# Gate units of a two-block transformer kernel computed in pairs by seven quarter products

## The chip, the cores and the metric

The kernel runs on one core of one Trainium2 chip. The metric is device time in microseconds, the median of several executions. The core's engines run side by side, each with its own queue of instructions, and wait for each other on semaphores: TensorE (PE in the profile; its weight loads are PEld), VectorE (DVE), ScalarE (ACT), GpSimd (POOL) and SyncE (SP), which issues the transfers of the weights.

## The reference, cut to what matters

Two transformer blocks run one after the other on 512 tokens of width 1024: a first block (stick-breaking attention, cross-attention, convolutional feed-forward) and a second with three branches (an RWKV-7 recurrence, a short convolution, a pooling). Only the end of the second block is touched. There `p_gate` holds 3 x 1024 columns of `h @ w_in`:

```python
y_a, v_layer = rwkv7_branch(...)
y_b = short_conv_branch(p_conv, conv_w[l])
y_c = pool_branch(p_pool, pool_w[l], pool_scale[l])
ys = jnp.stack([y_a, y_b, y_c], axis=0)
proj = jnp.einsum('nbsc,ncd->nbsd', ys, w_branch[l])
gates = jax.nn.sigmoid(p_gate.reshape(bsz, slen, N_BRANCH, D_MODEL))
merged = jnp.einsum('bsnd,nbsd->bsd', gates, proj)
out = merged @ w_out[l]
x = x + rms_norm(out, post_norm_w[l])
```

## The kernel before

**Tiles and units.** Activations lie transposed, features on the 128 partitions and the 512 tokens along the free dimension: `x_hi` and `x_lo` are eight such blocks. A *unit* is the weights of 128 output features, 1024 input rows deep, as a tile of 128x1024 (512 KB). 217 units are read in the order of their use, unit `u` into place `u % 4` of `stage`. SyncE issues the transfer of unit `u` when TensorE has finished unit `u - 4` (line 516).

**Three products for one.** Everything is split in two fp32r parts to keep fp32 accuracy. ScalarE rounds half a unit (128x512) from `stage` to `w_hi` (`split_hi`, line 1448). GpSimd subtracts (`split_lo`, line 2075) and writes `w_lo`, which lies at the same address as `stage`: the remainder replaces the weights. `product` (lines 562 to 564) then issues for each of a unit's eight blocks `w_lo` with `x_hi`, `w_hi` with `x_lo`, `w_hi` with `x_hi`, 24 matmuls of 512 columns into one bank of PSUM.

**The end of the second block.** After the recurrence come sixteen units "conv" (lines 1340 to 1342), eight units "pool", thirty-six units "branch" and eight units "out". VectorE makes the convolution's result (`conv_out`, lines 2825 to 2833), and for "pool" a windowed sum by doublings (lines 2877 to 2881); TensorE multiplies that with a small matrix (`mix`, line 1386, an fp32 product that the trace shows as x2), VectorE scales it (`pool_out`, line 2865), ScalarE rounds it (`pool_hi`, line 1993) and GpSimd makes the remainder (`pool_lo`, line 2240).

The branch stage has twelve steps, three branches by four pairs of output tiles. A step has three units: two gate units (output features `2m` and `2m + 1`), whose results ScalarE turns into `gates` by a sigmoid (line 2015), and one unit that holds both tiles' branch weights (24 matmuls, lines 1417 to 1419). VectorE multiplies gate and projection (line 2896) and adds to `Y` (line 2899). In the last four steps ScalarE rounds finished tiles of `Y` (`merged_hi`, line 2027) and GpSimd makes their remainders (`merged_lo`, line 2257) for "out". The first two units of "out" are computed interleaved, block by block (`two_products`, lines 579 to 592), so both must be ready when "out" begins.

Each engine's order is its program, written by hand as below. ScalarE splits unit `b + d + 2` ahead of the sigmoid of unit `b + d`; GpSimd goes through the units in order, three ahead.

## Time and profile before

| | |
|---|---|
| three runs | 1420.45, 1421.04, 1421.90 us; median 1421.04 us |
| span of the profiled execution | 1418.9 us, first to last instruction |
| TensorE busy | 1399.4 us, 99% |
| GpSimd, VectorE, ScalarE busy | 757.9, 666.8, 657.0 us |
| branch stage | about 1166 to 1363 us |

The profiled execution's own device time isn't listed. Its span is 2.1 us under the median of the runs, which is what lies around the span. Percentages of busy time are means over stages that differ much: TensorE is busy throughout, while the others wait for it for long in the branch stage.

### The profile page before, as it was taken

How to read it: one execution, taken by the hardware profiler on the slowest of the kernel's cores; microseconds unless marked ns; L12 is line 12 of the kernel's file. 1: busy time of each engine (PE TensorE's matmuls, PEld its weight loads, DVE VectorE, ACT ScalarE, POOL GpSimd, SP SyncE). 2: the span in 40 equal slices, each digit the busy share in tenths (PEclk: the TensorE clock that was granted, in tenths of full speed). 3: DMA queues.
4: the chain of work that ended last, by engine and by line, in shares of the span. 5: the costliest groups of instructions: out<-in, count | busy, mean ns of one | idle time of the engine just before them, and what ended most of it. 6: DMA issues, size and time to landing. Idle time of an engine off the chain costs nothing.

```text
span 1418.9 us, 23591 instructions
## 1 busy us (share of the span) xinstructions
PE 1399.4 (99%) x9244; PEld 1158.8 (82%) x9244; DVE 666.8 (47%) x857; ACT 657.0 (46%) x1138; POOL 757.9 (53%) x601
## 2 busy tenths in 40 slices
PE   8999999999999999999999999999999999999998
PEld 6888888787889888888888887788878878888887
DVE  5566655547646433333454875544355352111222
ACT  6555555535446544443332467456553333222343
POOL 4444433356346665656666545954337645445562
PEclk9999999999999999999999999999999999999999
DMA  5222222132131222232333312200023322323232
GB/s 211 90 88 77 87 75 84 65 104 75 60 134 45 80 99 98 95 99 94 105 104 104 119 45 89 75 19 3 3 74 120 103 89 89 105 89 104 89 103 75
DMA packets 34218, 122.99 MB, mean 87 GB/s; under 512 B 3792, under 2 KB 4304, under 8 KB 34000
## 3 DMA queue, kind: packets, MB, share of 16 engines
q1 hardware_dynamic: 33408, 119.51, 25.0%
q10 hardware_dynamic: 720, 2.20, 0.4%
q8 instruction: 67, 1.10, 0.3%
q14 instruction: 23, 0.19, 0.0%
HBM read 119.59 MB, written 2.10 MB: 86 GB/s over the span
## 4 chain that ended last, share of the span: by engine, by line
PE 87%; DVE 5%; issue 3%; ACT 3%; POOL 1%; DMA 0%; SPq 0%; POOLq 0%; ACTq 0%; DVEq 0%
PE ps L562 18%; PE ps L563 18%; PE ps L564 18%; PE ps L1340 2%; PE ps L1341 2%; PE ps L1342 2%; PE ps L1419 2%; PE ps L1418 2%; PE ps L1417 2%; PE ps L684 1%; PE ps L669 1%; POOL w_lo L2075 1%; PE ps L697 1%; PE ps L1106 1%; PE ps L849 1%
## 5 line engine op out<-in xcount | busy, mean ns | idle before, releaser
L2075 POOL TENSOR_TENSOR w_lo<-stage,w_hi 128x512 fp32r<-128x512 f32 x422 | 592.3, 1427 | 495.2 <-ACT w_hi L1448 495.1
L562 PE MATMUL ps<-x_hi,w_lo 128*128 128x512 f32 x888 | 349.6, 394 | 0.0
L564 PE MATMUL ps<-x_hi,w_hi 128*128 128x512 f32 x888 | 346.0, 390 | 0.0
L563 PE MATMUL ps<-x_lo,w_hi 128*128 128x512 f32 x888 | 345.8, 389 | 0.0
L1448 ACT ACTIVATE w_hi<-stage 128x512 fp32r<-128x512 f32 x422 | 241.6, 622 | 61.5 <-DMA stage<-w 53.8
L562 PEld LDWEIGHTS ps<-x_hi,w_lo 128*128 128x128 f32 x888 | 166.7, 188 | 36.6 <-issue 1.2
L564 PEld LDWEIGHTS ps<-x_hi,w_hi 128*128 128x128 f32 x888 | 166.7, 188 | 34.9
L563 PEld LDWEIGHTS ps<-x_lo,w_hi 128*128 128x128 f32 x888 | 166.8, 188 | 34.7 <-issue 1.2
L2567 DVE SCALAR_TENSOR_TENSOR conv<-ps,vcol,conv 128x511 f32<-128x511 f32 x44 | 33.0, 749 | 132.8 <-ACT conv L1668 132.8
L1668 ACT ACTIVATE conv<-ps,vcol 128x512 f32<-128x512 f32 x44 | 34.2, 778 | 121.4 <-PE ps L564 120.4
L2896 DVE TENSOR_TENSOR bt<-gates,ps 128x512 f32<-128x512 f32 x24 | 16.3, 679 | 141.5 <-PE ps L1419 141.5
L2015 ACT ACTIVATE gates<-ps 128x512 f32<-128x512 f32 x24 | 14.3, 597 | 114.2 <-PE ps L564 114.2
L562 PE MATMUL ps<-f_hi,w_lo 128*128 128x512 f32 x154 | 59.9, 389 | 0.0
L563 PE MATMUL ps<-f_lo,w_hi 128*128 128x512 f32 x154 | 59.9, 389 | 0.0
L564 PE MATMUL ps<-f_hi,w_hi 128*128 128x512 f32 x154 | 59.9, 389 | 0.0
L2115 POOL TENSOR_TENSOR f_lo<-conv,f_hi 128x512 f32 (+1 forms) x22 | 28.5, 1296 | 43.9 <-ACT f_hi L1680 43.9
L1340 PE MATMUL ps<-x_hi,w_lo 128*128 128x512 f32 x128 | 51.1, 400 | 0.1
L1341 PE MATMUL ps<-x_lo,w_hi 128*128 128x512 f32 x128 | 49.8, 389 | 0.0
L1342 PE MATMUL ps<-x_hi,w_hi 128*128 128x512 f32 x128 | 49.8, 389 | 0.0
L2187 POOL TENSOR_TENSOR Mk<-blk,levels 128x256 f32<-128x256 f32 x40 | 28.5, 728 | 38.1 <-PE ps L1276 17.4
L2319 DVE SCALAR_TENSOR_TENSOR keep<-ps,soft 128x1280 f32<-128x1280 f32 x16 | 23.8, 1490 | 42.5 <-ACT soft L1494 42.2
L1417 PE MATMUL ps<-ys_hi,w_lo 128*128 (+1 forms) x96 | 37.8, 393 | 0.0
(476 smaller groups left out, 2862.3 us busy)
## 6 DMA issues: line engine op xcount, KB each, us to landing
stage<-w SPq DMA_DIRECT2D x211, 512.0 KB, 3.3
extra_stage<-w SPq DMA_DIRECT2D x6, 512.0 KB, 5.1
H<-xT SPq DMA_DIRECT2D x4, 512.0 KB, 7.3
mem<-memT SPq DMA_DIRECT2D x2, 512.0 KB, 10.8
pool_n<-pool_count ACTq DMA_DIRECT2D x1, 1024.0 KB, 5.5
outT<-outs SPq DMA_DIRECT2D x4, 256.0 KB, 2.4
outT<-outs SPq DMA_DIRECT2D x2, 384.0 KB, 3.0
w_small<-small ACTq DMA_DIRECT2D x1, 512.0 KB, 5.8
```

Of the source, the lines that this page charges most:

```text
L562: pe.matmul(out, wl, hi(k), start=first, stop=False)
L563: pe.matmul(out, wh, lo(k), start=False, stop=False)
L564: mm = pe.matmul(out, wh, hi(k), start=False, stop=end)
L1340: pe.matmul(o, wl, x_hi[:, k, :], start=(k == 0), stop=False)
L1341: pe.matmul(o, wh, x_lo[:, k, :], start=False, stop=False)
L1342: mm = pe.matmul(o, wh, x_hi[:, k, :], start=False, stop=(k == KB - 1))
L1417: pe.matmul(o, wl, hi, start=(k == 0), stop=False)
L1448: act.activation(unit_hi(b)[:, cols], unit_stage(b)[:, cols], ACT.Copy).then_inc(whi_made, 1)
L1668: act.activation(conv[:, t % UP_BANKS, :], ps[:, t % UP_BANKS, :], ACT.Identity, scale=V("ffn_conv", (4 + t % 2) * FFB + p), bias=V("ffn_c ...
L2075: pool.tensor_tensor(unit_lo(b)[:, cols], unit_stage(b)[:, cols], unit_hi(b)[:, cols].bitcast(F32), ALU.subtract).then_inc(wlo_made, 1)
L2115: pool.tensor_tensor(f_lo[:, p, :], conv[:, slot, :], f_hi[:, p, :].bitcast(F32), ALU.subtract).then_inc(ff_made, 1)
L2567: dve.scalar_tensor_tensor(out=conv[:, j, 1:SEQ], in0=ps[:, j, 0:SEQ - 1], scalar=tap(1), in1=conv[:, j, 1:SEQ], op0=ALU.mult, op1=ALU.add ...
```

## The change

The two gate units of a step are one product of 256 output features, 1024 inputs and 512 tokens. The change cuts it in quarters: the weights by output tile and by half of the inputs (A11 and A12 are the halves of the first unit, A21 and A22 of the second), `x` by half of the inputs and half of the tokens. Eight quarter products are replaced by seven (the form of Strassen's scheme with fifteen sums), each four blocks deep and 256 columns wide.

- Four sums of `x` (`t_val`, `t_hi`, `t_lo`, 128x1024 each) are made once, in the conv stage: eight operations and four remainders on VectorE, four roundings on ScalarE.
- For each pair VectorE makes four 128x512 sums of weights (`pair_sums`), one of them in place in `stage`. ScalarE rounds three of them and GpSimd makes their remainders (`sum_hi`, `sum_lo`). The half A11, whose remainder overwrites `stage`, waits for the third sum.
- Three intermediate results are copied from PSUM to `gates` by ScalarE between the quarter products. VectorE adds the last parts (`gate_out`, `gate_out2`), and the sigmoid then works in place.
- The sequence of splits follows the pairs: the gate units of a pair are split only when their sums are made, one pair ahead, and the first pair after the pool stage. Other units are split as before.
- Some buffers move (`pool_n`, `sg`, `mg_hi`, `mg_lo`; `pt` and `pld` go into `cb`), and semaphores of the first stages are merged to free some; these wait for the same events as before.

```diff
+            def gate_pair(p, b, i=0, first=False):
...
+                if first:
+                    pe.wait_ge(pl_out_s, CA - 1)
+                pe.wait_ge(st_out_s, 8 * i + (2 * p + 2))
+                pe.wait_ge(wlo_made, 24 * i + (2 * b + 1))
+                seventh(B, hi0[:, left], lo0[:, left], *x_quarter(0, 0), start=True).then_inc(st_done_s, 1)
+                pe.wait_ge(wlo_made, 24 * i + (2 * b + 2))
...
+                seventh(Dq, hi1[:, right], lo1[:, right], *t_quarter(3), start=True)
                 if first:
                     mix(CA - 1)
+                pe.wait_ge(st_lo_s, 12 * i + (3 * p + 1))
+                n = s_place(0, p)
+                seventh(Cq, s_hi[n], s_lo[n], *t_quarter(0)).then_inc(st_done_s, 1)
+                pe.wait_ge(wlo_made, 24 * i + (2 * b + 3))
+                seventh(A, hi0[:, right], lo0[:, right], *x_quarter(1, 0), start=True).then_inc(unit_done, 1)
...
+                seventh(B, s_hi[n], s_lo[n], *t_quarter(1)).then_inc(st_done_s, 1)
...
+                seventh(Cq, s_hi[n], s_lo[n], *x_quarter(1, 1)).then_inc(st_done_s, 1)
+                pe.wait_ge(wlo_made, 24 * i + (2 * b + 4))
+                pe.wait_ge(st_copy_s, 12 * i + (3 * p + 3))
+                seventh(B, hi1[:, left], lo1[:, left], *t_quarter(2)).then_inc(unit_done, 1)
...
-                    split_hi(b + 2)
+                    if j < CA - 1:
+                        split_hi(b + 2)
...
+                if j == 13:
+                    for n in range(4):
+                        act.wait_ge(t_made_s, n + 1)
+                        act.activation(t_hi[n][:], t_val[n][:], ACT.Copy).then_inc(t_hi_s, 1)
...
+            def step(m, p, first=False):
...
+                act.activation(gates[:, g, 0:HS], quarter[:, 4, :], ACT.Copy).then_inc(st_copy_s, 1)
+                split_hi(b + 2)
...
+                act.activation(gates[:, g + 1, :], ps[:, 1, :], ACT.Copy).then_inc(st_copy_s, 1)
                 if first:
                     pool_hi(CA - 1)
...
+                act.activation(gates[:, g, HS:SEQ], quarter[:, 4, :], ACT.Copy).then_inc(st_copy_s, 1)
...
+                pair_hi(b + 3, 0)
+                pair_hi(b + 4, 1)
+                gate(m, p, 0)
+                sum_hi(0, p + 1)
+                sum_hi(1, p + 1)
+                pair_hi(b + 3, 1)
+                gate(m, p, 1)
+                sum_hi(2, p + 1)
+                third_hi(b + 4, p + 1)
...
+            def pair_los(p):
+                pair_lo(p, 0)
+                pair_lo(p, 1)
+                sum_lo(0, p)
+                pair_lo(p, 2)
+                sum_lo(1, p)
+                sum_lo(2, p)
+                pair_lo(p, 3)
...
             for m in range(4):
...
+                split_lo(U0["branch"] + 24 + 3 * m + 2)
+                if m < 3:
+                    pair_los(2 * QB + m + 1)
+                else:
+                    split_lo(U0["out"])
+                for k in range(2 * m - 2, 2 * m):
+                    if k >= 0:
+                        merged_lo(k)
+            split_lo(U0["out"] + 1)
             for k in range(KB - 2, KB):
                 merged_lo(k)
...
+            conv_out(1)
+            t_sums()
+            conv_out(2)
+            t_lows()
+            conv_out(3)
...
+            def pair_sums(p):
...
+                dve.wait_ge(whi_made, 2 * u + 2)
+                if p:
+                    dve.wait_ge(st_done_s, 4 * (p - 1) + 4)
+                dve.tensor_tensor(S1, A21, A22, ALU.add).then_inc(st_sum_s, 1)
+                dve.wait_ge(st_sum_s, 4 * p + 1)
+                dve.tensor_tensor(A21, A11, A21, ALU.subtract).then_inc(st_sum_s, 1)
+                dve.tensor_tensor(S2, S1, A11, ALU.subtract).then_inc(st_sum_s, 1)
+                dve.wait_ge(st_sum_s, 4 * p + 3)
+                dve.tensor_tensor(S4, A12, S2, ALU.subtract).then_inc(st_sum_s, 1)
...
+            for p in range(3 * QB):
+                gate_out(p)
+                if p < 3 * QB - 1:
+                    pair_sums(p + 1)
+                gate_out2(p)
+                taken(p)
```

**ScalarE at the end of the pool stage.** `sg<-ps` is the result of the last pool unit, `ys_hi<-cb` the rounding of the third pooled block (`pool_hi(2)`), which waits for VectorE's `pool_out` (`pl_out`). Before:

```order
L1448 ACTIVATE w_hi_51<-stage_50 128x512
L1453 ACTIVATE cb_178<-ps 128x512 [waits unit_done]
L1448 ACTIVATE w_hi_51<-stage_50 128x512 [waits landed2]
L1448 ACTIVATE w_hi_51<-stage_50 128x512
L2005 ACTIVATE sg_179<-ps 128x512 [waits unit_done]
L1993 ACTIVATE ys_hi_176<-cb_178 128x512 [waits gn_lo,pl_out]
L1448 ACTIVATE w_hi_51<-stage_50 128x512 [waits landed3]
```

After:

```order
L1514 ACTIVATE cb_178<-ps 128x512 [waits unit_done,pl_lo]
L2071 ACTIVATE sg_179<-ps 128x512 [waits unit_done]
L2058 ACTIVATE ys_hi_176<-cb_178 128x512 [waits gn_lo,pl_out]
L2079 ACTIVATE w_hi_51<-stage_50 128x512 [waits landed1]
L2079 ACTIVATE w_hi_51<-stage_50 128x512 [waits landed2]
L2085 ACTIVATE s_hi0_195<-s_val0_203 128x512 [waits st_sum]
L2085 ACTIVATE s_hi1_196<-s_val1_204 128x512 [waits st_sum]
L2079 ACTIVATE w_hi_51<-stage_50 128x512 [waits landed1]
```

The splits of the first two gate units stood ahead of `sg`; they now stand behind `ys_hi`, in four pieces with the sums' roundings between them.

**GpSimd in the last steps and ahead of "out".** `mg_lo` is the remainder of two tiles of `Y`, `w_lo` that of weights (two rows make a unit). Before, from the first `mg_lo` to the end:

```order
L2257 TENSOR_TENSOR mg_lo_184<-Y_55,mg_hi_183 128x512 [waits mg_hi_made] x2
L2075 TENSOR_TENSOR w_lo_49<-stage_50,w_hi_51 128x512 [waits whi_made] x6
L2257 TENSOR_TENSOR mg_lo_184<-Y_55,mg_hi_183 128x512 [waits mg_hi_made] x2
L2075 TENSOR_TENSOR w_lo_49<-stage_50,w_hi_51 128x512 [waits whi_made] x6
L2257 TENSOR_TENSOR mg_lo_184<-Y_55,mg_hi_183 128x512 [waits mg_hi_made] x4
L2075 TENSOR_TENSOR w_lo_49<-stage_50,w_hi_51 128x512 [waits whi_made] x12
```

After, from the last of the remainders of pair 10 on (two rows of L2190 are a whole unit; L2372 and L2380 are the seven pieces of pair 11):

```order
L2399 TENSOR_TENSOR mg_lo_182<-Y_55,mg_hi_181 128x512 [waits mg_hi_made] x2
L2190 TENSOR_TENSOR w_lo_49<-stage_50,w_hi_51 128x512 [waits whi_made] x2
L2372 TENSOR_TENSOR w_lo_49<-stage_50,w_hi_51 128x512 [waits st_sum,whi_made] x2
L2380 TENSOR_TENSOR s_lo0_199<-s_val0_203,s_hi0_195 128x512 [waits st_sum,st_hi]
L2372 TENSOR_TENSOR w_lo_49<-stage_50,w_hi_51 128x512 [waits st_sum,whi_made]
L2380 TENSOR_TENSOR s_lo2_201<-s_val2_205,s_hi2_197 128x512 [waits st_sum,st_hi]
L2380 TENSOR_TENSOR s_lo3_202<-s_val3_206,s_hi3_198 128x512 [waits st_sum,st_hi]
L2372 TENSOR_TENSOR w_lo_49<-stage_50,w_hi_51 128x512 [waits st_sum,whi_made]
L2399 TENSOR_TENSOR mg_lo_182<-Y_55,mg_hi_181 128x512 [waits mg_hi_made] x2
L2190 TENSOR_TENSOR w_lo_49<-stage_50,w_hi_51 128x512 [waits whi_made] x4
L2399 TENSOR_TENSOR mg_lo_182<-Y_55,mg_hi_181 128x512 [waits mg_hi_made] x2
L2190 TENSOR_TENSOR w_lo_49<-stage_50,w_hi_51 128x512 [waits whi_made] x2
```

Two `mg_lo` now stand ahead of the remainders of a pair's branch unit (the first and the ninth row), and the remainders of the second unit of "out" (the last row) stand behind the third pair of `mg_lo`; before they stood ahead of it.

## Rows read from the trace of the kernel before

**Rows 1.** The page: busy time of engines, and the chain that ended last.

```profile
PE 1399.4 (99%) x9244; PEld 1158.8 (82%) x9244; DVE 666.8 (47%) x857; ACT 657.0 (46%) x1138; POOL 757.9 (53%) x601
PE 87%; DVE 5%; issue 3%; ACT 3%; POOL 1%; DMA 0%; SPq 0%; POOLq 0%; ACTq 0%; DVEq 0%
```

**Rows 2.** Busy time by stretch: start:end, length, busy (instructions) of PE, PEld, DVE, ACT, POOL, granted clock.

```profile
1177.00:1363.00 186.00, 186.00 (x820) 153.68 (x820) 39.20 (x46) 54.08 (x98) 94.77 (x75) 1.00 0.29 96
1415.00:1416.00 1.00, 0.00 (x0) 0.00 (x0) 0.26 (x1) 0.38 (x1) 0.00 (x0) 1.00 0.73 279
...
1418.00:1419.00 1.00, 0.00 (x0) 0.00 (x0) 0.00 (x0) 0.00 (x0) 0.00 (x0) 0.63 0.00 1
```

**Rows 3.** Timeline of PE, 512 columns: first and last of a step's 48 gate matmuls.

```profile
1183.39 0.39 PE L562 MATMUL ps<-x_hi,w_lo 128*128 128x512 f32 x1
...
1194.05 0.39 PE L564 MATMUL ps<-x_hi,w_hi 128*128 128x512 f32 x1
```

**Rows 4.** The same, 256 columns: first and last of 36 matmuls.

```profile
785.77 0.28 PE L1035 MATMUL ps<-f_hi,w_lo 128*128 128x256 f32 x1
...
789.97 0.28 PE L1037 MATMUL ps<-f_hi,w_hi 128*128 128x256 f32 x1
```

**Rows 5.** PE, DVE, ACT and POOL where the pool stage ends.

```profile
1165.26 1.02 PE L1386 MATMUL ps<-pld,w_small 128*128 128x512 f32 x2
1165.71 0.80 PE L562 MATMUL ps<-x_hi,w_lo 128*128 128x512 f32 x1
1160.65 0.15 DVE L2877 COPY pt<-cb 128x1 f32<-128x1 f32 x1 [4.93 <-ACT cb L1453]
1167.75 0.74 DVE L2865 SCALAR_TENSOR_TENSOR cb<-ps,vcol,sg 128x512 f32<-128x512 f32 x1
1168.53 0.63 ACT L1993 ACTIVATE ys_hi<-cb 128x512 fp32r<-128x512 f32 x1 [2.47 <-DVE cb L2865]
1169.06 1.14 ACT L1448 ACTIVATE w_hi<-stage 128x512 fp32r<-128x512 f32 x2
1161.21 2.77 POOL L2075 TENSOR_TENSOR w_lo<-stage,w_hi 128x512 fp32r<-128x512 f32 x2 [0.17 <-ACT w_hi L1448]
```

**Rows 6.** SP and ACT: two gate units' transfers, from issue to the split.

```profile
1194.65 0.33 SPq L516 DMA_DIRECT2D stage<-w  x1
1197.99 1.15 ACT L1448 ACTIVATE w_hi<-stage 128x512 fp32r<-128x512 f32 x2 [1.82 <-DMA stage<-w]
...
1210.94 0.33 SPq L516 DMA_DIRECT2D stage<-w  x1
1214.67 1.15 ACT L1448 ACTIVATE w_hi<-stage 128x512 fp32r<-128x512 f32 x2 [2.18 <-DMA stage<-w]
```

**Rows 7.** POOL remainders alone and beside DVE, and DVE beside them.

```profile
1180.85 5.05 POOL L2075 TENSOR_TENSOR w_lo<-stage,w_hi 128x512 fp32r<-128x512 f32 x4
1124.65 5.94 POOL L2075 TENSOR_TENSOR w_lo<-stage,w_hi 128x512 fp32r<-128x512 f32 x4 [0.74 <-ACT w_hi L1448]
1127.78 1.66 DVE L2880 TENSOR_TENSOR pld<-pt,pool_n 128x512 f32<-128x512 f32 x1
1219.10 0.69 DVE L2899 TENSOR_TENSOR Y<-Y,bt 128x512 f32<-128x512 f32 x1
```

**Rows 8.** Groups by shape: sigmoid and 128x256 copies on ACT, 128x1024 on DVE.

```profile
L2015 ACT ACTIVATE gates<-ps 128x512 f32<-128x512 f32 x24 | 14.3, 597 | 114.2 <-PE ps L564 114.2
L1926 ACT ACTIVATE R<-ps 128x256 f32<-128x256 f32 x31 | 11.5, 385 | 13.0 <-PE ps L1276 7.1 <-PE ps L1295 4.8
L2427 DVE TENSOR_TENSOR prob<-prob,soft_sum 128x1024 f32<-128x1024 f32 x4 | 4.9, 1225 | 0.1
```

**Rows 9.** Conv stage: DVE's gap, POOL beside it, and PE at unit 12.

```profile
1093.56 0.72 DVE L2825 TENSOR_TENSOR cb<-cb 128x512 f32<-128x512 f32 x1 [14.54 <-ACT cb L1947]
1086.62 4.61 POOL L2234 TENSOR_TENSOR ys_lo<-g_sq,ys_hi 128x2048 fp32r<-128x2048 f32 x1
1098.16 0.39 PE L1340 MATMUL ps<-x_hi,w_lo 128*128 128x512 f32 x1
```

More of the change, by code:

```diff
@@ L369, in build_block @@
         xa_max = sem("xa_max")
-        xa_nmax = sem("xa_nmax")
         xa_exp = sem("xa_exp")
@@ L1396, in _, with seventh @@
                     mix(j - 1)
-            def step(n, m, b, i=0, first=False):
-                for d in range(2):
-                    pe.wait_ge(evac, 8 * i + (EV0["branch"] + 2 * ((b - U0["branch"]) // 3) + d + CREDIT - 1))
-                    product(ps[:, (U0["branch"] + d) % 2, :], 12 * i + (b + d), (b + d) % RING, x_rows, x_rows_lo)
+            def seventh(out, wh, wl, hi, lo, start=False):
+                for k in range(QB):
+                    cols = slice(k * P, (k + 1) * P)
+                    pe.matmul(out, wl[:, cols], hi(k), start=start and k == 0, stop=False, skip_group_check=True)
+                    pe.matmul(out, wh[:, cols], lo(k), start=False, stop=False, skip_group_check=True)
+                    mm = pe.matmul(out, wh[:, cols], hi(k), start=False, stop=(k == QB - 1), skip_group_check=True)
+                return mm
@@ new lines, in x_quarter, with t_quarter @@
+            def x_quarter(r, c):
+                return lambda k: x_hi[:, QB * r + k, HALF[c]], lambda k: x_lo[:, QB * r + k, HALF[c]]
+            def t_quarter(n):
+                return lambda k: t_hi[n][:, k, :], lambda k: t_lo[n][:, k, :]
+            def gate_pair(p, b, i=0, first=False):
+                left, right = (slice(0, UNIT // 2), slice(UNIT // 2, UNIT))
+                hi0, lo0, hi1, lo1 = (t[:, (b + d) % RING, :] for d in range(2) for t in (w_hi, w_lo))
+                A, Dq, Cq, B = (quarter[:, n, :] for n in (1, 2, 3, 4))
+                if first:
[4 more added lines that the diff above has]
+                pe.wait_ge(wlo_made, 24 * i + (2 * b + 2))
+                if first:
+                    pe.wait_ge(t_lo_s, 4)
+                    pe.wait_ge(evac, EV0["branch"] + CREDIT)
+                seventh(Dq, hi1[:, right], lo1[:, right], *t_quarter(3), start=True)
@@ L1406, in step @@
+            def step(n, m, b, i=0, first=False):
+                gate_pair(m, b, i, first)
                 st = (b - U0["branch"]) // 3
@@ L2016, in step @@
                 if first:
                     pool_hi(CA - 1)
-                split_hi(b + 4)
-            for m in range(4):
-                step(m, U0["branch"] + 3 * m, first=m == 0)
-            for m in range(4):
-                step(m, U0["branch"] + 12 + 3 * m)
+                act.wait_ge(st_done_s, 4 * p + 3)
+                act.activation(gates[:, g, HS:SEQ], quarter[:, 4, :], ACT.Copy).then_inc(st_copy_s, 1)
+                if not more:
+                    split_hi(b + 3)
+                    gate(m, p, 0)
+                    gate(m, p, 1)
+                    split_hi(b + 4)
+                    return
@@ L2025, in merged_hi @@
+            third_hi(b + 1, 0)
+            act.wait_ge(pl_pooled_s, CA)
+            for p in range(2 * QB):
+                step(p % QB, p, first=p == 0)
             def merged_hi(k):
@@ new lines, in gate_out, with gate_out2 @@
+            def gate_out(p):
+                g = 2 * (p % 2)
+                dve.wait_ge(st_done_s, 4 * p + 4)
+                dve.wait_ge(st_copy_s, 3 * p + 3)
+                g0 = gates[:, g, :].rearrange("p (h n) -> p h n", n=HS)
+                dve.tensor_tensor(g0, g0, quarter[:, 1:4:2, :], ALU.add).then_inc(st_out_s, 1)
+            def gate_out2(p):
+                g1 = gates[:, 2 * (p % 2) + 1, :].rearrange("p (h n) -> p h n", n=HS)
+                dve.wait_ge(unit_done, U0["branch"] + 3 * p + 2 + CREDIT)
+                dve.tensor_tensor(g1, g1, quarter[:, 4:5, :].to_broadcast([P, 2, HS]), ALU.add).then_inc(st_out_s, 1)
@@ L2903, in _ @@
-            with dve.Fori(1, 3) as i:
-                for m in range(4):
-                    step(m, U0["branch"] + 3 * m, i)
+            for p in range(3 * QB):
[4 more added lines that the diff above has]
+                taken(p)
             dve.memset(acc2[:], 0.0).then_inc(acc2_made, 1)
```

220 lines of the change are left out of this document (144 added, 76 removed).

## Prediction, made before the changed kernel was run

> **What bounds the kernel now.** First the page: TensorE is busy for 99% of the span and has 87% of the chain that ended last [rows 1], so a saved matmul counts fully as long as nothing comes late. Then the stretches: in the branch stage TensorE is busy without a gap, GpSimd for 95 us of 186, ScalarE and VectorE for less [rows 2]. So there is room beside TensorE, but room in a mean says nothing about lateness. For that I follow one step by the timeline. Last I look at the two ends of the stage, where the new preparation has no earlier pair to hide behind.
>
> The profiled execution has a span of 1418.9 us, 2.1 under the median. I work on the span and add the difference to the median, 1421.04.
>
> **What goes.** A step's gate units are 48 matmuls of 512 columns; from the first to the last, 47 intervals take 10.66 us, 0.2268 each, so 10.89 for the pair [rows 3]. The new pair is seven quarters of four blocks by three products, 84 matmuls of 256 columns. 36 of this kernel's present 256-column matmuls, with their weight loads, start 0.1200 apart [rows 4]: 10.08 us, 1.44 a quarter. That gains 0.81 a pair, 9.7 us for twelve. It isn't an eighth of 10.89 since a narrow matmul costs more than half of a wide one. A step shrinks from 16.33 to 15.52, the branch unit's 24 matmuls staying at 5.44.
>
> **The steady step** (time 0 is a pair's first quarter). ScalarE's roundings cost 0.57 to 0.62 each, GpSimd's remainders 1.263 (5.05 for four), VectorE's sums 0.69 and 0.04 between two [rows 5, 7].
> The next pair's second unit takes the place that the fourth quarter frees. A transfer is issued 0.60 after the start of the last matmul [rows 3, 6], 0.11 less with the shorter matmul: 6.13. It is being rounded 3.34 to 3.73 after the issue [rows 6]: 9.6, rounded at 10.2. VectorE needs the sixth quarter's result for `gate_out` by then (8.9 to 9.6), fits, and makes three sums: 12.4. Only now may GpSimd overwrite A11: it starts at 12.5 and has nine operations to the end of the next branch unit's remainders, 11.4 us: 23.9.
> VectorE's operations with two SBUF inputs and GpSimd's hinder each other: 0.69 became 1.66 beside GpSimd, and GpSimd's four took 5.94 for 5.05, 0.45 for each of the two VectorE operations within them [rows 7]. Three such (the fourth sum, two additions to `Y`) make 25.2. The branch unit begins at 15.52 + 10.08 = 25.60. The first remainder is ready at 13.8 to 14.2 for 15.52, and the later ones come every 1.26 to 1.7 for quarters of 1.44. So a steady step is hidden by 0.4 us at its tightest place. ScalarE's third copy, which the seventh quarter waits for, has one quarter, 1.44, for 0.39 [rows 8] and about 0.3 of waiting. I charge 1.0 for eleven steps, bounds 0 and 3 (a transfer at 3.73 in each and one more collision in some).
>
> **The first pair.** Before, ScalarE split both gate units ahead of the pool stage's last results. Now they stand behind `ys_hi`. Reckoned: the fp32 `mix` ends at 1166.28; `pool_out` takes 0.74 (VectorE is done with its doublings by then, since GpSimd's 2.77 us of splits beside them go: about 2.0 earlier), `ys_hi` 0.63, two half units 1.14, three sums 2.2, a remainder 1.27, with 0.05 to 0.1 for each handing over: 1172.5 to 1173.2 [rows 5, 7]. The upper end has a sum behind `ys_lo` and the remainder behind the fourth sum. TensorE had its first gate matmul behind `mix` at 1166.3. Stall: 6.2 to 6.9, I take 6.5. Nothing hides it; the quarter waits for these weights alone.
> The first branch unit's remainders stand behind the seven pieces and `pool_lo(3)`: 1172.6 + 7 x 1.27 + 1.3 + 2.5 = 1184.0 for 1183.7 (10.08 and 0.86 for `mix` on): 0.3, bounds 0 and 0.6.
>
> **The clock in that stall.** The trace has one long idleness of TensorE, the tail: no matmul runs from 1415.0 on, and the granted clock of 1418 to 1419 is 0.63 on average [rows 2], so within it the clock went from 2.4 GHz to 1.2 GHz. An idleness of 6.5 us is longer. I count on the fall. How long the low level then lasts isn't in these rows. At one end it costs nothing, at the other half of the first pair's 10.08 us runs at half rate, 5. I take 1.5, near the lower end, since the pair's pieces come only every 1.27 us and the waits 0.3 above would take up a part.
> The Trainium skill, "TensorE: Matmul & The Clock Gate", Part 1, says that idleness lowers the clock and that only sustained work releases it again. By that rule the term can't be zero; without it the sum below would be 1424.7. The rule speaks against this change, which makes the kernel's first long idleness in the middle of its work.
>
> **The last pairs.** Pairs are counted from 0 to 11. Behind the pieces of pairs 10 and 11 GpSimd makes two remainders of `Y` ahead of the branch unit's: 2.53 more, 27.7 for 25.6. The branch product of step 10 waits 2.1 (bounds 1.7 and 2.6). The one of step 11 gains from it: TensorE is 2.1 later, GpSimd's chain began before the wait, so it is late by about 0.
> Ahead of "out": the seventh quarter ends at 10.3, `gate_out2` 11.0, sigmoid 11.65, the split of the second unit of "out" 12.8, two tiles of `Y` rounded 13.4 and 14.1. GpSimd has its two `mg_lo` to 16.0 and then the second unit's halves: 18.6, and 0.45 to 0.9 more beside VectorE's last additions. "out" begins at 15.52 and asks for both halves 0.45 later. Late by 2.4 to 3.5; I take 3.0. Before, this split stood first.
>
> **The sums of x.** VectorE has a gap of 14.5 us behind `conv_out(1)` [rows 9]. Eight sums of 128x1024 at 1.23 [rows 8] are 9.8 alone and up to 19 beside GpSimd. Each holds GpSimd up by about 0.9; its unit 12, behind the 4.61 us remainder of `g_sq`, then ends near TensorE's start of that unit, 1098.16 [rows 9]. Charged 0.5, bounds 0 and 2.5. ScalarE's four roundings (about 1 us each) and the four `t_lo` delay `conv_out(3)` by a microsecond or two, which the pool stage's gaps of 4.9 us on VectorE take up [rows 5]. Semaphores merged and buffers moved: nothing, their waits are on the same events.
>
> **The sum.** -9.7 + 6.5 + 0.3 + 1.5 + 1.0 + 2.1 + 3.0 + 0.5 = +5.2: 1426.2 us. All terms at their lower ends give +0.6 (1421.6), all at their upper ends +14.4 (1435.4).
>
> **The rivals.**
> *Near break-even, 1422.* The same stalls at their lower ends, the clock returned at once: +0.6 to +2.8. For it: the tight places are tight by tenths. Against: four terms would have to be low together.
> *Faster, 1417.9.* GpSimd isn't late at the end: the place is its queue from pair 10 on, the price 2.1 + 3.0 of my sum. It decides if the nine remainders and two `mg_lo` end before 25.6, so if its chain starts 2.1 earlier than 12.5, that is if the second unit's weights are there at 8.1 instead of 10.2. Then only the join is left: -9.7 + 6.2 + 0.3 = -3.2. Against: transfers of 3.3 us or more in every step [rows 6].
> *Collisions in every step, 1433.* VectorE's four sums all collide and the branch product is late by 0.7 in each of the steps not yet counted: +7. Against: GpSimd is idle when the first three sums run.
> *The change doesn't do what it says, 1430.* If the narrow matmuls with new groups started 0.125 apart the gain would be 4.7. Against: [rows 4], whose weights change with each matmul too.
>
> **How the numbers follow.** This kernel's measurement tells about 0.2%, 2.8 us, from no change: 1418.2 to 1423.9 is "same". My forecast has 0.54, break-even 0.21, faster 0.11, collisions 0.09, the weaker gain 0.05. Slower by over 0.2%: 0.54 + 0.09 + 0.05 = 0.68, same 0.21, faster 0.11. Range 1418.5 to 1431.5: it leaves out most of the faster case and the upper part of the collisions.
>
> **What would show it.** In the trace after: quarter matmuls 0.120 apart, 1.44 a quarter; one idle stretch of TensorE of 6 to 7 us released by GpSimd's first `w_lo` of the branch stage, and a clock under 1.00 in or behind it; steps of 15.5 us; a wait of 2 us at the branch product of step 10 and one near 3 us at the second unit of "out"; next to nothing in the conv stage. It would be wrong if the gap at the join is short, if steady steps show waits of GpSimd's, or if the clock stays low for long.

## The result, and the profile after

The changed kernel takes 1427.93 us (median of 4 runs, 1427.56 to 1429.48) and the kernel before 1420.74 us (1419.9 to 1421.9). The ratio is 1.0053, with a 95% interval of 1.0038 to 1.0067: slower by about half a per cent. The medians differ by 7.2 us. The prediction said 1426.2 us, 1418.5 to 1431.5, slower with a chance of 0.68. The profiled execution spans 1425.6 us, 6.7 more than the 1418.9 of before.

First the page: busy time by engine, and under it the chain that ended last.

```profile
PE 1395.2 (98%) x9676; PEld 1175.5 (82%) x9676; DVE 749.9 (53%) x941; ACT 697.4 (49%) x1214; POOL 828.8 (58%) x637
PE 90%; DVE 4%; POOL 2%; ACT 2%; issue 1%; DMA 1%; SPq 0%; ACTq 0%; POOLq 0%; DVEq 0%
```

Against [rows 1]: TensorE is busy for only 4.2 us less, though the quarter products save over 9 (most of the rest is work at a lower clock, as shown below). VectorE is busy for 83 us more and GpSimd for 71. GpSimd's share of the chain is 2%, where it was 1%. Where GpSimd is waited for, the waits of TensorE say (engine, tile and line <- what it waited for: us in total, times, longest), from 1000 us to the end:

```profile
PE ps L1419 <- POOL w_lo L2372: 6.7, 1, 6.7
PE ps L607 <- POOL w_lo L2190: 2.6, 1, 2.6
PE ps L1478 <- POOL w_lo L2190: 2.1, 1, 2.1
```

All three are new, and each is for a remainder of GpSimd's: at the first pair (L1419), at the second unit of "out" (L607), and at the branch product of step 10 (L1478). Nothing else in the branch stage waits, in the steady steps not once. The steps, from the timeline of TensorE (start, duration, engine and line, tiles, in brackets the idleness before it), are the first quarter matmul of a pair (L1419) or the first of a branch unit (L1478), and last the one of "out" that waits (L607):

```profile
1221.52 0.28 PE L1419 MATMUL ps<-x_hi,w_lo 128*128 128x256 f32 x1
...
1231.59 0.40 PE L1478 MATMUL ps<-ys_hi,w_lo 128*128 128x512 f32 x1
...
1237.06 0.28 PE L1419 MATMUL ps<-x_hi,w_lo 128*128 128x256 f32 x1
...
1342.59 0.50 PE L1478 MATMUL ps<-ys_hi,w_lo 128*128 x1 [2.06 <-POOL w_lo L2190]
...
1349.78 0.28 PE L1419 MATMUL ps<-x_hi,w_lo 128*128 128x256 f32 x1
...
1368.54 0.79 PE L607 MATMUL ps<-mg_hi,w_lo 128*128 128x512 f32 x1 [2.60 <-POOL w_lo L2190]
```

A pair takes 1231.59 - 1221.52 = 10.07 us, the branch unit 5.47, the step 15.54 where it was 16.32. So each steady step is a gain, of 0.78 us. But the branch unit of step 10 takes 7.19 us from its first matmul to the next pair, 1.7 more than its sisters. The granted clock tells why. Windows of one microsecond with TensorE alone (start:end, length, busy share and matmuls, granted clock, DMA share, GB/s), around step 10 and around the join:

```profile
1344.00:1345.00 1.00, 1.00 (x5) 0.54 0.00 0
1345.00:1346.00 1.00, 1.00 (x4) 0.50 0.00 0
1346.00:1347.00 1.00, 1.00 (x3) 0.50 0.00 0
1347.00:1348.00 1.00, 1.00 (x5) 0.75 0.00 0
1348.00:1349.00 1.00, 1.00 (x6) 1.00 0.00 0
```

```profile
1169.00:1170.00 1.00, 0.00 (x0) 1.00 0.00 0
1170.00:1171.00 1.00, 0.00 (x0) 0.50 0.00 0
...
1175.00:1176.00 1.00, 1.00 (x7) 0.50 0.00 0
1176.00:1177.00 1.00, 1.00 (x7) 0.58 0.00 0
1177.00:1178.00 1.00, 1.00 (x5) 1.00 0.00 0
```

At the join the clock is at the lower of its two levels (0.50 is 1.2 GHz) from 1170 us, still within the wait, to 1176.9; TensorE works again from 1171.72. The pair takes 13.25 us to its branch unit, where 10.08 and 0.86 for the pool product are 10.94: 2.3 us more. At step 10 the fall comes 1.5 us behind the wait's end, when TensorE is already busy again. At "out" there is a third one: it comes at 1368.0, in the last half microsecond of the wait, and lasts to 1371.4; the stretch from the first product of "out" to the end takes 60.28 us for 55.99 before, of which 2.6 are the wait and 1.7 the clock.

The join itself, answering [rows 5], with all engines (the order is that of the chain):

```profile
1164.03 1.02 PE L1402 MATMUL ps<-cb,w_small 128*128 128x512 f32 x2
1165.09 0.75 DVE L3035 SCALAR_TENSOR_TENSOR cb<-ps,vcol,sg 128x512 f32<-128x512 f32 x1 [0.50 <-PE ps L1402]
1165.87 0.63 ACT L2058 ACTIVATE ys_hi<-cb 128x512 fp32r<-128x512 f32 x1 [1.05 <-DVE cb L3035]
1166.41 1.13 ACT L2079 ACTIVATE w_hi<-stage 128x512 fp32r<-128x512 f32 x2
1167.57 0.82 DVE L3063 TENSOR_TENSOR s_val<-stage 128x512 f32<-128x512 f32 x1 [1.73 <-ACT w_hi L2079]
1169.87 2.94 POOL L2372 TENSOR_TENSOR w_lo<-stage,w_hi 128x512 fp32r<-128x512 f32 x2 [2.02 <-DVE s_val L3066]
1171.72 0.55 PE L1419 MATMUL ps<-x_hi,w_lo 128*128 128x256 f32 x1 [6.67 <-POOL w_lo L2372]
```

Scaling, `ys_hi`, two half units, three sums, remainder: one after the other, as the prediction had it, and TensorE beside it idle.

### The profile page after: what moved, and what is told of

The parts are those of the page before. It is cut to its first block, busy times and chain, and to the rows that moved or that the text cites. A ratio compares the mean times of both kernels' runs of the same rounds, so it can differ in the third digit from the quotient of the medians.

```text
span 1425.6 us, 24785 instructions
## 1 busy us (share of the span) xinstructions
PE 1395.2 (98%) x9676; PEld 1175.5 (82%) x9676; DVE 749.9 (53%) x941; ACT 697.4 (49%) x1214; POOL 828.8 (58%) x637
## 4 chain that ended last, share of the span: by engine, by line
PE 90%; DVE 4%; POOL 2%; ACT 2%; issue 1%; DMA 1%; SPq 0%; ACTq 0%; POOLq 0%; DVEq 0%
PE ps L578 16%; PE ps L579 16%; PE ps L580 16%; PE ps L1419 3%; PE ps L1420 3%; PE ps L1421 3%; PE ps L1356 2%; PE ps L1358 2%; PE ps L1357 2%; PE ps L1478 1%; PE ps L1479 1%; PE ps L1480 1%; PE ps L685 1%; PE ps L713 1%; PE ps L700 1%; PE ps L950 1%
## 5 line engine op out<-in xcount | busy, mean ns | idle before, releaser
L2190 POOL TENSOR_TENSOR w_lo<-stage,w_hi 128x512 fp32r<-128x512 f32 x374 | 541.3, 1472 | 401.8 <-ACT w_hi L1509 401.6
L578 PE MATMUL ps<-x_hi,w_lo 128*128 128x512 f32 x696 | 274.6, 395 | 0.0
L580 PE MATMUL ps<-x_hi,w_hi 128*128 128x512 f32 x696 | 271.3, 390 | 0.0
L579 PE MATMUL ps<-x_lo,w_hi 128*128 128x512 f32 x696 | 271.1, 390 | 0.0
L1509 ACT ACTIVATE w_hi<-stage 128x512 fp32r<-128x512 f32 x374 | 214.0, 622 | 48.3 <-DMA stage<-w 38.1
L578 PEld LDWEIGHTS ps<-x_hi,w_lo 128*128 128x128 f32 x696 | 130.7, 188 | 28.9 <-issue 1.1
L580 PEld LDWEIGHTS ps<-x_hi,w_hi 128*128 128x128 f32 x696 | 130.6, 188 | 27.6
L579 PEld LDWEIGHTS ps<-x_lo,w_hi 128*128 128x128 f32 x696 | 130.7, 188 | 26.8 <-issue 1.0
L2372 POOL TENSOR_TENSOR w_lo<-stage,w_hi 128x512 fp32r<-128x512 f32 x48 | 67.9, 1426 | 31.7 <-DVE s_val L3066 31.7
L2380 POOL TENSOR_TENSOR s_lo<-s_val,s_hi 128x512 fp32r<-128x512 f32 x36 | 53.8, 1508 | 0.0
L1356 PE MATMUL ps<-x_hi,w_lo 128*128 128x512 f32 x128 | 51.2, 400 | 0.1
L1358 PE MATMUL ps<-x_hi,w_hi 128*128 128x512 f32 x128 | 49.9, 390 | 0.0
L1357 PE MATMUL ps<-x_lo,w_hi 128*128 128x512 f32 x128 | 49.8, 389 | 0.0
L2463 DVE SCALAR_TENSOR_TENSOR keep<-ps,soft 128x1280 f32<-128x1280 f32 x16 | 23.9, 1491 | 42.3 <-ACT soft L1555 42.1
L1478 PE MATMUL ps<-ys_hi,w_lo 128*128 (+1 forms) x96 | 38.3, 399 | 2.1 <-POOL w_lo L2190 2.1
```

The source lines that it names most:

```text
L578: pe.matmul(out, wl, hi(k), start=first, stop=False)
L579: pe.matmul(out, wh, lo(k), start=False, stop=False)
L580: mm = pe.matmul(out, wh, hi(k), start=False, stop=end)
L1356: pe.matmul(o, wl, x_hi[:, k, :], start=(k == 0), stop=False)
L1357: pe.matmul(o, wh, x_lo[:, k, :], start=False, stop=False)
L1358: mm = pe.matmul(o, wh, x_hi[:, k, :], start=False, stop=(k == KB - 1))
```

## The experiments

All are the changed kernel with one edit or several, timed beside the kernel before, in 4 to 11 executions each. They ran on two chips, and each ratio is to the kernel before on the same chip. The changed kernel itself stands at 1.0053 on this scale, and 0.1% are 1.4 us. **Theory:** the whole loss is three waits, at the two ends of the stage, and the clock's falls behind them; the steady step is the gain that it seems. **Rivals:** the cost is spread (operations of VectorE and GpSimd that hinder each other in every step), or the waits are there whatever the order, since GpSimd has too much to do.

| kernel | median, us | ratio to before, 95% | against the changed kernel | theory |
|---|---|---|---|---|
| e_out_first | 1423.89 | 1.0024 (1.0015 to 1.0033) | -4.1 | -4.3 |
| e_merged_gap | 1428.82 | 1.0061 (1.0048 to 1.0074) | +1.1 | -3.8 |
| e_join_early | 1428.13 | 1.0055 (1.0042 to 1.0068) | +0.3 | -7.8 |
| e_warm_join | 1424.85 | 1.0036 (1.0023 to 1.0049) | -2.4 | -2.3 |
| e_join2 | 1418.68 | 0.9985 (0.9976 to 0.9994) | -9.7 | -7.7 |
| e_tail | 1420.76 | 1.0004 (0.9995 to 1.0013) | -7.0 | -8.0 |
| e_all2 | 1413.52 | 0.9947 (0.9933 to 0.996) | -15.1 | -15.7 |
| e_pool_extra | 1430.1 | 1.0068 (1.0053 to 1.0084) | +2.1 | +5.4 |

The fourth column is the difference of the ratios, in microseconds of 1420.7. The changed kernel's own ratio is known to 0.15% either way, so such a difference is good to some 2.5 us: +0.3, +1.1, -2.4 and +2.1 aren't clear of nothing by the time alone, and what is said of these four rests on their traces.

### The second unit of "out" first (e_out_first)

```diff
                 else:
                     split_lo(U0["out"])
+                    split_lo(U0["out"] + 1)
                 for k in range(2 * m - 2, 2 * m):
                     if k >= 0:
                         merged_lo(k)
-            split_lo(U0["out"] + 1)
```

> One change to the changed kernel: GpSimd splits the second unit of "out" directly behind the first, ahead of its four merged_lo remainders of k = 4 to 7, as the kernel before did. In the changed kernel's trace TensorE waits 2.6 us for that unit's w_lo, and its granted clock is 0.50 in the three microseconds behind the wait; from the first product of "out" to the end takes 60.28 us, 4.29 more than before. Theory (the wait and the clock fall behind it are one cost of the order on GpSimd): both go, 60.3 falls to 56.0 to 56.6, the whole to 1423.3 to 1424.2 us. Rival (the remainders mg_lo become the late ones in its place): the wait moves to mg_lo, at least 2 us of the 4.3 stay, and the whole is 1426 or more.

The theory held: -4.1 us for the expected -4.3. From the first product of "out" to the end this trace takes 56.0 us, as before the change, and the granted clock is 1.00 for as long as TensorE works there. No remainder became late in the unit's place. So the wait at "out" came of the place of one line, not of GpSimd's load.

### The merged remainders into the idle stretch (e_merged_gap)

```diff
                 split_lo(U0["branch"] + 24 + 3 * m + 2)
+                for k in range(2 * m - 4, 2 * m - 2):
+                    if k >= 0:
+                        merged_lo(k)
                 if m < 3:
                     pair_los(2 * QB + m + 1)
                 else:
                     split_lo(U0["out"])
-                for k in range(2 * m - 2, 2 * m):
-                    if k >= 0:
-                        merged_lo(k)
+            for k in range(KB - 4, KB - 2):
+                merged_lo(k)
             split_lo(U0["out"] + 1)
```

> One change to the changed kernel: in the last block's third and fourth steps GpSimd computes the merged remainders that ScalarE has made ready in the step before (k = 0, 1 and 2, 3) in its own idle stretch, directly behind the branch unit's split, and no longer between the pair's remainders and the next branch unit. In the changed kernel's trace the branch product of step 10 waits 2.06 us for its w_lo, and takes 7.19 us where the others take 5.47, at a granted clock of 0.50. Theory: the wait and the slow product both go, 3.8 us, and the stretch from the end of the pool stage to "out" is 197.5 us where it was 201.29; the whole 1424 us. Rival (a wait of 2.1 us is too short to bring the clock down, and the slow product comes of something else, say the port): 2.1 us go, the product stays at 7.2, the whole 1425.9. Second rival (the two remainders don't fit into the gap, 3.0 us, and delay the next pair): nothing is gained.

Nothing was gained, but not for the reason that any of the three gives. The waits of TensorE in its trace:

```profile
PE ps L1419 <- POOL w_lo L2372: 6.7, 1, 6.7
PE ps L607 <- POOL w_lo L2190: 4.6, 1, 4.6
PE ps L1478 <- POOL w_lo L2190: 0.6, 2, 0.4
```

The wait at step 10 is gone (the 0.6 us are 0.2 at step 1 and 0.4 at step 11), so the remainders do fit into the gap. But TensorE now reaches "out" 2 us sooner, and the unit it needs there comes when it came: the 2.6 us became 4.6, with the clock down behind it for longer. GpSimd works there without a gap from 1345.55, where pair 11's pieces begin, to 1369.04, where that unit's remainders are done: work taken out of step 10 stands in the same queue ahead of "out". The two waits at the end are one debt, and to remove the earlier alone moves it.

### Both orders (e_tail)

```diff
                 split_lo(U0["branch"] + 24 + 3 * m + 2)
+                if m == 2:
+                    merged_lo(0)
+                    merged_lo(1)
                 if m < 3:
                     pair_los(2 * QB + m + 1)
                 else:
                     split_lo(U0["out"])
-                for k in range(2 * m - 2, 2 * m):
-                    if k >= 0:
-                        merged_lo(k)
             split_lo(U0["out"] + 1)
-            for k in range(KB - 2, KB):
+            for k in range(2, KB):
                 merged_lo(k)
```

> The two orders on GpSimd together, since e_merged_gap's trace shows the wait that it took from step 10 (2.06 to 0 us) come back whole at the second unit of "out" (2.6 to 4.6 us): both are one chain on GpSimd. Here the remainders of k = 0, 1 go into the idle stretch of the third step, and those of k = 2 to 7 stand behind both of the first units of "out". Theory (all that TensorE waits for at the end is this order): step 10's 2.06 us and its clock's 1.7 go, as do the 2.6 us at "out" and its clock's 1.6; 8.0 us less than the changed kernel, 1419.9 us, which is level with the kernel before. Rival (GpSimd has too much work in this stretch whatever its order: some remainder or the third unit of "out" is late): 2 to 4 us of it stay, 1422 to 1424 us.

The theory held: of the 8.1 us that the two waits and the clock behind each cost in the trace of after (2.06 + 1.7 + 2.6 + 1.7), it returned 7.0. The only wait left there is 0.3 us. So GpSimd had the time; and the kernel is level with before while the join still costs it 6.7 us and the clock's fall.

### The clock kept up in the join (e_warm_join)

```diff
                 if first:
+                    for k in range(26):
+                        pe.matmul(ps[:, 7, :], x_hi[:, k % KB, 0:P], x_hi[:, k % KB, :], start=True, stop=True)
                     pe.wait_ge(pl_out_s, CA - 1)
```

> One change to the changed kernel: TensorE runs 26 matmuls of 512 columns (x_hi by itself, into bank 7, whose values nobody reads) where it waits for the first pair, 26 x 0.227 = 5.9 of the 6.67 us. No wait is removed: the first pair's w_lo comes when it comes. In the changed kernel's trace the granted clock is 0.50 in the six microseconds behind that wait and the pair takes 13.25 us from its first product to the branch unit, where 12 x 7 x 0.120 + 0.86 for the pool product is 10.9. Theory (the clock's fall is a cost of its own, 2.3 us): the granted clock stays at 1.00, the pair takes 11.0 us, the whole is 1425.6 us. Rival (the first pair is slow because its operands come late one by one, whatever the clock): the clock stays, and the pair takes 13 us still, the whole 1427.9.

It came out as the theory had it: the clock stays at 1.00, and the pair takes 11.24 us for 13.25, though not one operand comes earlier. The time is 2.4 us less for the expected 2.3. The idleness costs TensorE twice, once as a wait and once as a clock. The five executions spread widely, from 1422.1 to 1428.2 us. The one of the trace is the fastest, and no wait in it is followed by a fall; the slowest has the lowest mean clock, 0.997. This trace showed something more. Here is its step 10, whose wait is 2.00 us and ends at 1340.52, and the clock behind it:

```profile
1340.00:1341.00 1.00, 0.48 (x2) 1.00 0.93 344
1341.00:1342.00 1.00, 1.00 (x6) 1.00 0.29 115
...
1344.00:1345.00 1.00, 1.00 (x6) 1.00 0.00 0
```

No fall, for nearly the same wait as in the trace of after. Of the six traces with a wait of 1.8 to 2.1 us at step 10, three have the fall (after, e_join_early, e_join2: 2.06, 2.01 and 2.05 us) and three have none (e_out_first, e_warm_join, e_pool_extra: 1.94, 2.00 and 1.80). By these six alone it could be the length, for the three longest have the fall. The waits at "out" speak against it: of three of 2.60 and 2.61 us, only the one in after has a fall, and those in e_join_early and e_join2 have none. A wait of two or three microseconds may or may not bring the clock down; what decides isn't settled by these runs.

### The first pair prepared early (e_join_early, e_join2)

```diff
# ScalarE, pool stage
             for j in range(CA):
+                if j == CA - 1:
+                    pair_hi(U0["branch"], 0)
+                    pair_hi(U0["branch"] + 1, 1)
+                    sum_hi(0, 0)
+                    sum_hi(1, 0)
...
                     else:
+                        if j == CA - 1:
+                            pair_hi(U0["branch"], 1)
+                            sum_hi(2, 0)
+                            third_hi(U0["branch"] + 1, 0)
# GpSimd
+                    if j == CA - 1 and c == 0:
+                        pair_los(0)
                     if j and c == 0:
                         pool_lo(j - 1)
# VectorE
             for j in range(CA):
+                if j == CA - 1:
+                    pair_sums(0)
                 src = cb[:, j % 2, 0, :]
```

(The same calls behind the loops are gone.)

> One change to the changed kernel: the first pair's rounding (ScalarE), sums (VectorE) and remainders (GpSimd) are issued ahead of the last channel's work in the pool stage, where the changed kernel's trace shows all three idle between 1155 and 1159 us, and no longer behind it. TensorE then waits only for the pool stage's last scaling of bank 2 (VectorE L3035, from 1165.09 to 1165.84, some 1.2 us after the last product ends). Theory (the join's 6.67 us wait is nothing but this preparation, and the clock at 0.50 for six microseconds behind it is the wait's consequence): the wait falls from 6.7 to about 1.2 us and the clock doesn't fall: 5.5 + 2.3 = 7.8 us less, the whole 1420.2 us, level with the kernel before. Rival (preparing beside the pool stage collides: VectorE's pooling sums and GpSimd's seven remainders in 1156 to 1166 us make the last channel's work late): 3 us or more of the wait stays, the whole over 1423.

The rival won outright. TensorE waits 8.1 us, and not for a remainder:

```profile
1164.97 1.73 DVE L3066 TENSOR_TENSOR cb<-cb 128x510 f32<-128x510 f32 x1
1166.73 1.11 DVE L3065 COPY cb<-cb 128x4 f32<-128x4 f32 x1
...
1170.76 1.70 DVE L3066 TENSOR_TENSOR cb<-cb 128x504 f32<-128x504 f32 x1
...
1173.83 0.74 DVE L3036 SCALAR_TENSOR_TENSOR cb<-ps,vcol,sg 128x512 f32<-128x512 f32 x1
...
1174.68 0.55 PE L1419 MATMUL ps<-x_hi,w_lo 128*128 128x256 f32 x1 [8.06 <-issue]
```

The pair's sums are done at 1162, its remainders at 1172. But beside these remainders a pooling addition takes 1.7 us for 0.69, and a copy of four columns 1.11 for 0.17. The pooling ends at 1173.9, and the scaling that empties bank 2 stands behind it in VectorE's order (L3036), for which the first quarter product waits. The Trainium skill, "SBUF — State Buffer", in the section "SBUF: two separate sides", says that a VectorE operation with two SBUF inputs, or one in a 2-port mode, such as a fp32 copy within SBUF, and a GpSimd operation take the shared ports in turn, each for its whole length. The trace agrees: additions and copies alike lose about a microsecond beside operations of 1.3 us. The next kernel puts this scaling ahead of the last channel's pooling, and the last pool product behind the sixth quarter:

```diff
# VectorE
                 if j == CA - 1:
                     pair_sums(0)
+                    pool_out(j - 1)
...
                 gate_out(p)
+                if p == 0:
+                    pool_out(CA - 1)
# TensorE, gate_pair
-                if first:
-                    mix(CA - 1)
                 pe.wait_ge(st_lo_s, 12 * i + (3 * p + 1))
...
                 pe.wait_ge(st_copy_s, 12 * i + (3 * p + 3))
+                if first:
+                    mix(CA - 1)
```

(With it, `pool_hi` and `pool_lo` of the last channel move behind the second pair's first roundings and the first branch unit's remainders, and ScalarE rounds the first pair ahead of its wait for `pool_lo`.)

> The first pair is prepared early, as in e_join_early, whose trace shows what made that one gain nothing: VectorE's pooling sums of the last channel, 0.69 us each alone, took 1.70 to 1.73 us each beside GpSimd's seven remainders, the pooling ended at 1173.9 us where it had ended at 1164.6, and the last scaling of bank 2, for which the first quarter product waits, stood behind it. Here two places are changed: VectorE scales bank 2 ahead of the last channel's pooling sums, and these then run beside TensorE's first pair, with the last pool product moved to before the pair's seventh product; GpSimd's remainders run ahead of them. Theory (the join costs only what stands ahead of the first product, and the collision was the rival's whole strength): TensorE waits about 1.3 us, the clock stays, 5.4 + 2.3 = 7.7 us less than the changed kernel, 1420.2 us. Rival (the last channel's pooling, now beside the pair, is late for the sums of the second pair, and the wait comes back at the second pair): 3 us or more of it stays, over 1423 us.

-9.7 us for the expected -7.7, so the kernel is 0.15% faster than before with the end's faults still in it. TensorE waits 0.9 us ahead of the pair and 0.8 at the pool product within it, at a clock of 1.00. The pooling is as slow as in e_join_early (1.74 us an addition), and nobody waits for it beyond that 0.8: the same collision made over 7 us of wait in one order (8.1 for the 0.9 that are there without it) and under one in the other.

### Everything (e_all2)

The edits of e_join2 and e_tail together.

> e_join2 and e_tail together. Theory (the steady steps' gain of 0.78 us each is real and everything else was waits at the two ends): 7.7 + 8.0 = 15.7 us less than the changed kernel, 1412.2 us, 8 us under the kernel before. Rival (the gains at the two ends are taken back somewhere, as e_merged_gap's was): 1418 us or more.

The waits of TensorE in its trace, from 1000 us on:

```profile
PE ps L1402 <- DVE cb L3073: 0.9, 1, 0.9
PE ps L1419 <- issue: 0.9, 1, 0.9
PE ps L578 <- ACT Y L2161: 0.6, 1, 0.6
...
PE ps L1478 <- POOL w_lo L2193: 0.2, 1, 0.2
```

1413.52 us, 0.53% under the kernel before (interval 0.40 to 0.67), and faster than both. The parts add up within the noise (9.7 + 7.0 = 16.7, measured 15.1, each good to some 2.5): nothing is seen to be taken back. What is left of waits in the branch stage is 2.0 us (0.9, 0.9 and 0.2), and 9.4 less 2.0 is 7.4, near the 6.7 us by which the medians differ. So the seven quarter products are a gain of about 7 us, once little waits at their ends.

### One more operation on GpSimd in each steady step (e_pool_extra)

```diff
                 pool.wait_ge(st_sum_s, 4 * p + after)
+                if n == 2 and 0 < p < 10:
+                    pool.tensor_tensor(w_small[:, 0, :], stage[:, slot, cols], w_hi[:, slot, cols].bitcast(F32), ALU.subtract)
                 pool.tensor_tensor(w_lo[:, slot, cols], stage[:, slot, cols], w_hi[:, slot, cols].bitcast(F32),
```

> The changed kernel with one more 128x512 subtraction on GpSimd (1.29 us) in each of the pairs 1 to 9, written where nobody reads. It measures how near the steady step is to a wait: in the changed kernel's trace GpSimd ends the branch unit's remainders at 1230.9 and TensorE starts that unit at 1231.59, 0.7 us later; ahead of the pair it sits idle 3.0 us for the last weight sum. Theory (the cover in a steady step is 0.7 us, for the idle stretch lies ahead of a wait and can't be used): each of nine steps is 0.6 us longer, 5.4 us in all, 1433.3 us, with waits at the branch unit's w_lo (L1478); more if the clock falls in them. Rival (the idle 3.0 us are cover): no step is longer, 1427.9 us.

```profile
PE ps L1419 <- POOL w_lo L2374: 6.7, 1, 6.7
PE ps L1478 <- POOL w_lo L2190: 3.8, 7, 1.8
PE ps L607 <- POOL w_lo L2190: 1.3, 1, 1.3
```

The theory was right in kind, not in size. The steps do get longer and TensorE does wait at the branch units. From pair 1 to pair 10 it takes 143.9 us for nine times 15.54, 139.9: +4.1 us, of which the first of the nine has 0.9 and the others 0.39 each.

The cover isn't 1.29 - 0.39, though, since neighbouring steps share a shortage. GpSimd begins a pair's pieces 12.25 us after the start of the pair before (here 1219.60 for 1207.35, in after 1218.22 for 1205.98), however long TensorE waits at the branch unit in between. So a wait in one step is already won for the next. One step of this kernel, GpSimd's first and last operation and the branch unit:

```profile
1219.60 3.00 POOL L2374 TENSOR_TENSOR w_lo<-stage,w_hi 128x512 fp32r<-128x512 f32 x2 [2.02 <-DVE s_val L3068]
...
1230.96 2.55 POOL L2190 TENSOR_TENSOR w_lo<-stage,w_hi 128x512 fp32r<-128x512 f32 x2
1233.66 0.47 PE L1478 MATMUL ps<-ys_hi,w_lo 128*128 128x512 f32 x1 [0.15 <-POOL w_lo L2190]
```

GpSimd needs 13.9 us here for 12.7 in after, 1.2 more, and two steps together are 2 x 0.39 = 0.8 us longer: the cover is about 0.4. The trace of after says much the same directly: the remainders are ready 0.69 us ahead of the branch unit, of which the handing over takes 0.15, so 0.5. The expectation took the whole 0.7 and priced each step by itself. The idle 3.0 us aren't cover: they are 2.0 here, and the steps are longer all the same. The time shows only 2.1 us, with an interval of nearly 3 either way; this execution also had no fall of the clock at step 10 or "out", which the trace of after has.

## Why the prediction was right, term by term

| term | predicted | measured | from |
|---|---|---|---|
| seven quarters for eight | -9.7 | -9.4 | 12 x 0.78, steps |
| first pair's wait | +6.5 | +6.7 | waits |
| first branch unit | +0.3 | 0 | waits (0.3 in e_warm_join) |
| clock at the join | +1.5 | +2.3 | 13.25 for 10.94 |
| steady steps | +1.0 | 0 | waits |
| step 10: wait | +2.1 | +2.1 | waits |
| step 10: clock | none | +1.7 | 7.19 for 5.47 |
| "out": wait | +3.0 | +2.6 | waits |
| "out": clock | none | +1.7 | 60.28 - 55.99 - 2.6 |
| sums of x | +0.5 | +0.1 | conv stage, 102.3 for 102.2 |
| sum | +5.2 | +7.8 | span: +6.7 |

**The gain.** 84 matmuls 0.120 us apart, as [rows 4] said. That the quarters are narrow costs what it was said to, and the rival of 0.125 falls. (Its price was also off: 5.0 us less gain is 1431.2, not 1430.)

**The join.** The chain of [rows 5] came item by item, and 6.67 us lie in the bounds of 6.2 to 6.9. That the operations alone make it is shown by e_join2, where it falls to 0.9 us. The next term, the first branch unit's remainders, is written with seven pieces, which would give 1185.3; its 1184.0 is right for the six that stand behind the first remainder. In after that wait vanishes behind the slow clock. In e_warm_join, where the clock stays, the unit starts 0.3 us late, as reckoned.

**The clock.** This is the step that was mis-sized. The prediction counted one fall, the join's, with 1.5 us, and took a value near the lower end because the pair's pieces would hold TensorE up anyhow. In after they didn't: GpSimd was ahead of TensorE at half rate, and the pair took 2.3 us more than 10.94. That cost isn't a fixed one. In the four other traces with the same wait of 6.67 us (e_out_first, e_merged_gap, e_tail, e_pool_extra) the pair takes 13.57, 13.77, 12.27 and 12.32 us, so 1.3 to 2.8 more, and 1.5 lies within that. What failed is that two further falls, at waits of 2.1 and 2.6 us, weren't counted at all: [rows 2] show only that a long idleness brings a fall, and I took short ones to be free without a reason. Together the clock cost 5.7 us in after where 1.5 were reckoned. The Trainium skill, "TensorE: Matmul & The Clock Gate", Part 1, says that idleness lowers the clock and only sustained work releases it; the three falls agree, each with work at 0.50 behind it for some microseconds.

**The end.** In after, step 10 is 2.06 for 2.1, "out" 2.6 in a range of 2.4 to 3.5, and step 11 shows no wait, as the prediction had it. The faster rival falls with it. Part of this agreement is luck, for the fall at step 10, which wasn't reckoned, moves the other two. Where the clock stays at 1.00 behind step 10's wait (e_out_first, e_warm_join, e_pool_extra), step 11 waits 0.64 to 0.68 us, where about 0 was predicted. And "out" waits only 1.3 us in the two of them that keep its order, where 3.0 was. From e_warm_join:

```profile
1357.00 0.50 PE L1480 MATMUL ps<-ys_hi,w_lo 128*128 x1 [0.68 <-POOL w_lo L2192]
...
1364.46 0.50 PE L607 MATMUL ps<-mg_hi,w_lo 128*128 128x512 f32 x1 [1.28 <-POOL w_lo L2192]
```

From step 10's branch unit to this place in "out" it is 25.9 us in the three traces with the fall and 23.9 in these two: with what it moves, the fall costs 2.0 us. What the prediction didn't see either is that the waits at the end are one debt. It priced the faster rival as if 2.1 + 3.0 went together, which is right, but gave no price for one of them going alone: nil for the earlier (e_merged_gap), 4.1 us with its clock for the later (e_out_first).

**The steady step.** Predicted hidden by 0.4 at its tightest place, charged 1.0 to be safe; it is hidden by about 0.5 (after, e_pool_extra), and costs nothing. GpSimd in one step of after:

```profile
1218.22 2.99 POOL L2372 TENSOR_TENSOR w_lo<-stage,w_hi 128x512 fp32r<-128x512 f32 x2 [3.04 <-DVE s_val L3066]
1221.17 1.29 POOL L2380 TENSOR_TENSOR s_lo<-s_val,s_hi 128x512 fp32r<-128x512 f32 x1
1222.42 1.29 POOL L2372 TENSOR_TENSOR w_lo<-stage,w_hi 128x512 fp32r<-128x512 f32 x1
1223.67 3.46 POOL L2380 TENSOR_TENSOR s_lo<-s_val,s_hi 128x512 fp32r<-128x512 f32 x2
1227.09 1.30 POOL L2372 TENSOR_TENSOR w_lo<-stage,w_hi 128x512 fp32r<-128x512 f32 x1
1228.35 2.55 POOL L2190 TENSOR_TENSOR w_lo<-stage,w_hi 128x512 fp32r<-128x512 f32 x2
```

Nine operations in 12.7 us, with three collisions of about 0.45 (2.99 for 2.53, 3.46 for 2.53), as the sum had them. The pair starts at 1221.52, and both of its first remainders are there by 1221.21; the branch unit's are ready at 1230.90 for 1231.59. The rival of collisions in every step falls: VectorE's first three sums run in GpSimd's idle 3.04 us.

**The sums of x.** They took VectorE from 1077.58 to 1097.7, longer than reckoned (one of 128x1024 took 5.46 us beside GpSimd's 5.60 us remainder, where 1.2 is what it takes alone), and cost 0.1 us: from its first unit to the pool stage's first the conv stage takes 102.29 us (1016.41 to 1118.70) where it took 102.15 (1017.77 to 1119.92). The stage's own sums on VectorE have slack.

**The remainder.** 7.8 were added up, and the span rose by 6.7. The missing 1.1 us lie ahead of the branch stage, and of the conv stage too, which begins 1.4 earlier in after. The pool product behind the stage's last unit starts at 1164.03 in after and at 1165.26 in before [rows 5], 1.2 later. In the eight other kernels, whose instructions for TensorE are the same as after's up to there, it starts between 1163.87 and 1165.59. So executions differ by that much in the first 1160 us, and the trace of after is among the early ones. The median of all runs rose by 7.2.

That the forecast came so near is partly errors against each other: the clock was reckoned 4.2 us too low, everything else 1.6 too high, and this execution is 1.1 early.

## What to carry to other kernels

A step that pays in its steady state is only half of a change: count what the pipeline's first and last turns wait for, and order the helpers' work there by who is waited for, before judging the idea. Here the arithmetic gained 9.4 us and two ends lost 17; the same arithmetic with the helpers' work in another order is 0.5% faster than before. Waits behind one another on one queue can be one debt: removing the first alone gained nothing here. And a wait of TensorE's of 2 us or more can bring a fall of the clock with it. Here four of nine waits of 1.8 to 2.6 us did, each for 1.7 us more, and all seven of 4.6 us and longer; behind the join's that cost 1.3 to 2.8 us.
